# Heads between scores and probabilities, a section in two parts, scatters in parts, later small loads, output by halves

## The reference

```python
sh1, sc1, gt1, sh2, sc2, gt2 = split(silu(cond) @ w_mod[l] + b_mod[l], 6)
h = rmsnorm(x, g_mix[l]) * (1 + sc1) + sh1
aq, ak, av, mq, mk, mv, mo, mi, mf = split(h @ w_in[l])
att  = softmax(rope(norm(aq)) @ [cache_k, rope(norm(ak))].T / 8) @ [cache_v, av]   # 8 query, 2 key heads of 64
h_ml = mlstm_forward(mq, mk, mv, mi, mf) + mlstm_backward(...)                     # 4 heads of 128
x = x + gt1 * concat(att, sigmoid(mo) * rmsnorm(h_ml)) @ w_out[l]
h = rmsnorm(x, g_ffn[l]) * (1 + sc2) + sh2
gates = top-1 group of 4, then top-2 experts in it, of softmax(h @ w_router)
x = x + gt2 * sum_e gates_e * (silu(h @ w_gate[l,e]) * (h @ w_up[l,e])) @ w_down[l,e]   # 16 experts of 512
```

## Time and profile before

| | us |
|---|---|
| median of 3 runs | 891.59 (891.47 to 891.73) |
| the profiled execution | 891.36 |
| its span in the profile | 889.2 |
| PE busy | 837.6 (94% of the span) |
| DVE, ACT, POOL busy | 269.7, 179.6, 46.8 |
| chain that ended last: PE, DMA, DVE, ACT | 75%, 13%, 6%, 4% |

### The profile page before, as it was taken

How to read it: one execution, slowest core, us unless ns; L and a number is a source line. 1 busy time by engine, 2 the same in 40 slices (tenths; PEclk the granted TensorE clock), 3 DMA queues, 4 the chain that set the end, 5 groups by cost and what they waited for, 6 DMA issues and landing times.

```text
span 889.2 us, 10662 instructions
## 1 busy us (share of the span) xinstructions
PE 837.6 (94%) x4332; PEld 470.2 (53%) x4332; DVE 269.7 (30%) x503; ACT 179.6 (20%) x354; POOL 46.8 (5%) x51
## 2 busy tenths in 40 slices
PE   4899999998999999999989999989799999999996
PEld 3364647775444554355445555778553555345533
DVE  0211385425322122202230317652532022202222
ACT  3221224415101110011031212350510110011101
POOL 0400220101000000000000004000000000000000
PEclk9999999999999999999999999999699999999999
DMA  8995468859799999999999445705249999999981
GB/s 355 353 389 203 174 251 338 297 191 418 298 402 422 427 429 427 430 428 427 425 402 356 179 189 180 299 25 190 95 195 394 424 429 427 430 428 430 427 382 49
DMA packets 39763, 289.32 MB, mean 325 GB/s; under 512 B 3304, under 2 KB 5664, under 8 KB 21296
## 3 DMA queue, kind: packets, MB, share of 16 engines
q1 hardware_dynamic: 38000, 285.30, 78.9%
q0 software_dynamic: 1488, 3.44, 1.3%
q10 hardware_dynamic: 240, 0.08, 0.0%
HBM read 286.44 MB, written 2.37 MB: 325 GB/s over the span
## 4 chain that ended last, share of the span: by engine, by line
PE 75%; DMA 13%; DVE 6%; ACT 4%; issue 1%; SPq 1%; ACTq 0%; DVEq 0%
PE ps L965 22%; PE ps L639 13%; DMA ring<-in_w_e_up 10%; PE ps L993 9%; PE ps L885 6%; PE ps L953 6%; PE ps L1002 5%; DMA ring<-in_w_in 3%; PE ps L651 3%; PE ps L560 3%; PE ps L805 1%; PE ps L820 1%; ACT xe L1324 1%; DVE og L1543 1%; ACT hT L1150 1%
## 5 line engine op out<-in xcount | busy, mean ns | idle before, releaser
L965 PE MATMUL ps<-ring,xe 128*64 128x512 f32 x1024 | 223.5, 593 | 0.8 <-DMA ring<-in_w_e_up 0.6
L965 PEld LDWEIGHTS ps<-ring,xe 128*64 128x64 f32 x1024 | 75.2, 137 | 145.2 <-issue 145.0
L639 PE MATMUL ps<-ring,hT 128*128 128x512 f32 (+1 forms) x320 | 128.7, 563 | 4.1 <-DMA ring<-in_w_in 2.5
L993 PE MATMUL ps<-ring,hidT 128*64 128x512 f32 x512 | 113.4, 595 | 1.6 <-ACT hidT L1336 1.6
L639 PEld LDWEIGHTS ps<-ring,hT 128*128 128x128 f32 x320 | 62.1, 195 | 68.0 <-issue 59.1
L1754 DVE COPY ye<-ps 128x512 f32<-128x512 f32 x16 | 11.1, 692 | 215.0 <-PE ps L993 215.0
L953 PE MATMUL ps<-pick,htok 128*128 (+1 forms) x512 | 67.3, 288 | 7.4 <-ACT xe L1324 3.5
L993 PEld LDWEIGHTS ps<-ring,hidT 128*64 128x64 f32 x512 | 36.2, 137 | 67.4 <-issue 66.0
L953 PEld LDWEIGHTS ps<-pick,htok 128*128 128x128 f32 x512 | 64.1, 202 | 11.9 <-ACT xe L1324 6.8
L1002 PE MATMUL ps<-scat,ye 128*128 (+1 forms) x256 | 59.5, 385 | 1.8 <-DVE ye L1754 1.8
L1002 PEld LDWEIGHTS ps<-scat,ye 128*128 128x128 f32 x256 | 47.3, 190 | 20.6 <-issue 14.8
(11 more groups left out here) (258 smaller groups left out, 635.0 us busy)
## 6 DMA issues: line engine op xcount, KB each, us to landing
ring<-in_w_e_gate SPq DMA_DIRECT2D x32, 2048.0 KB, 13.9
ring<-in_w_e_up SPq DMA_DIRECT2D x32, 2048.0 KB, 17.0
ring<-in_w_e_down SPq DMA_DIRECT2D x32, 2048.0 KB, 12.1
ring<-in_w_mod SPq DMA_DIRECT2D x24, 2048.0 KB, 10.7
ring<-in_w_in SPq DMA_DIRECT2D x10, 2048.0 KB, 20.5
ring<-in_w_out SPq DMA_DIRECT2D x4, 2048.0 KB, 12.8
ring<-in_w_in SPq DMA_DIRECT2D x2, 1024.0 KB, 17.5
C<-in_state_C POOLq DMA_DIRECT2D x2, 512.0 KB, 7.6
```

Source lines behind the costliest of these rows:

```text
L639: mm = pe.matmul(bank[:, 0:width], hT[:, k, b * P:(b + 1) * P], w[:, k, :], start=(k == 0), stop=(k == KD - 1))
L965: mm = pe.matmul(ps[1 + u][64 * j:64 * j + 64, :], xe[:, k, j * SLOTS:(j + 1) * SLOTS], w[j][:, k, :], start=(k == 0), stop=(k == KD - 1))
L993: mm = pe.matmul(ps[3 - half][64 * j:64 * j + 64, :], hidT[:, k, j * SLOTS:(j + 1) * SLOTS], w[j][:, k, half * 512:(half + 1) * 512], star ...
```

## The change

1. The mLSTM heads move between the attention's scores and probabilities. On PE `own(0, 0..3)` comes ahead of the scores, `carried` and `own(1, .)` of heads 0 and 1 between s12 and s13, those of heads 2 and 3 behind the turned probabilities; `turn_heads(1)` and `turn_heads(0)` go behind the state, the second behind the fillers 6 and 7. DVE and ACT follow. The scaled `inter` values have three buffers in `hT` where they had two in `pT1`. The second reciprocal of DVE's gate goes behind `joined(3)`.
2. Layer 1's last section has two halves of 8 chunks: section 2 (scale 2) with two slots in the mixing stage (`filling` 0 and 4 only), and section 3 (gate 2) with two slots loaded behind `w_out` and used as filler in the router stage. An instruction is 256 wide instead of 512, and a slot has 16 instead of 8.
3. A scatter waits for the second half of ye only ahead of its fifth chunk; in the last pair its last two chunks go behind `turn_hidden`.
4. POOL's small loads wait for the first projection's weights instead of the fourth modulation slot. The first slot of section 0 is multiplied ahead of the norm sums.
5. The output is turned, copied and stored by halves of the features, four stores of 256 KB for two of 512 KB, the first halves as soon as two of the four residual parts are done.

The diff, cut to its core:

```diff
+SECTION_CHUNKS = {(l, s): (16 * s, 16) for l in range(DEPTH) for s in range(3)}
+SECTION_CHUNKS[1, 2], SECTION_CHUNKS[1, 3] = (32, 8), (40, 8)
+def section_slots(l, s):
+    return SECTION_CHUNKS[l, s][1] // 4
+def last_section(l):
+    return later_sections(l)[-1]
 def later_sections(l):
-    return ([(l, 1)] if l == 0 else []) + [(l, 2)] + ([(l + 1, 0)] if l + 1 < DEPTH else [])
+    return ([(l, 1)] if l == 0 else []) + [(l, 2), (l + 1, 0) if l + 1 < DEPTH else (l, 3)]
...
-        inter_s = pT1.ap().rearrange("p i j k t -> p (i j k t)")[:, 0:4 * (MD + 1)].rearrange("p (n d e) -> p n d e", n=2, d=2)
+        inter_s = hT.ap().rearrange("p k t -> p (k t)")[:, MH * TOK:MH * TOK + 6 * (MD + 1)].rearrange("p (n d e) -> p n d e", n=3, d=2)
...
@@ block.sync
-            for b, name in enumerate(("y_prompt", "y_sample")):
-                for half in range(2):
-                    taken(sp, ("out", 2 * b + half))
-                sp.dma_start(t[name][0], otok[:, b, :]).then_inc(y_out, 16)
+            for half in range(2):
+                for b, name in enumerate(("y_prompt", "y_sample")):
+                    taken(sp, ("out", 2 * half + b))
+                    c = slice(half * 512, half * 512 + 512)
+                    sp.dma_start(t[name][0][:, c], otok[:, b, c]).then_inc(y_out, 16)
@@ block.tensor
+                if l == 0:
+                    pe.wait_ge(cond_silu, 1)
+                    section_rows(0, 0, 0)
                 for i in range(4):
                     norm_sums(("ssq1", l), sq, 2 * l, (2 * i, 2 * i + 1), i == 0, i == 3)
...
-                        elif n % 2 == 0:
-                            section_rows(l, 2, n // 2)
+                        elif n in (0, 4):
+                            section_rows(l, 2, n // 4)
...
-                taken(pe, ("qT1", l), ("kT1", l))
-                for i in range(4):
+                for h in range(MH):
+                    own(0, h)
+                taken(pe, ("qT1", l), ("kT1", l))
+                for i in range(3):
+                    cross_scores(i)
+                if l == 0:
+                    section_columns(l, 1)
+                for h in range(2):
+                    carried(h)
+                    own(1, h)
+                cross_scores(3)
...
+                filling(5)
+                for h in range(2, MH):
+                    carried(h)
+                    own(1, h)
...
+                turn_heads(1)
                 filling(6, 7)
+                turn_heads(0)
...
-                if filler:
-                    section_rows(l + 1, 0, 0)
+                section_rows(*fill, 0)
                 pe.wait_ge(part_ready, l + 1)
...
-                        scatter(p - 1)
+                        scatter(p - 1, chunks=range(KD - 2 if last else KD))
                     turn_hidden(p)
-                    if not last:
+                    if last:
+                        scatter(p - 1, chunks=(KD - 2, KD - 1))
...
-            taken(pe, (("y", 3), DEPTH - 1))
             for r in range(4):
-                b, half = r // 2, r % 2
+                b, half = r % 2, r // 2
+                taken(pe, (("y", 2 * half + 1), DEPTH - 1))
@@ block.scalar
-                for i in range(6):
-                    exponent(i)
...
+                for i in range(3):
+                    exponent(i)
+                carry(0)
+                carry(1)
+                for i in range(3, 6):
+                    exponent(i)
...
+                for b in (1, 0):
+                    key = (f"oT{b}", l)
+                    bank = full(act, key)
+                    act.activation(cat[:, 0:4, b * P:(b + 1) * P], bank[:, :].rearrange("p (k t) -> p k t", k=4),
+                                   ACT.Copy).then_inc(free(key), 1)
                 act.activation(scrap[:, :], eps[:, :], ACT.Ln)
@@ block.vector
+                score_peaks(0, 1, 2)
+                if l == 0:
+                    modulation_columns(l, 1)
+                open_gate(1, 0, ML // 2)
+                score_peaks(3, 4, 5)
+                joined(0)
+                joined(1)
                 taken(dve, (("num", 0, MH - 1), l))
                 divisors(0)
-                joined(0)
-                joined(1)
+                 heads_out(0).then_inc(head_sum, 1)
                 joined(2)
                 joined(3)
+                open_gate(1, ML // 2, ML)
+                attended(1)
                 taken(dve, (("num", 1, MH - 1), l))
                 divisors(1)
...
                 dve.tensor_reduce(hr[:, 1, :], num[:, 1, :, 0, 0:MD], AX_X, ALU.add).then_inc(head_ssq, 1)
+                attended(0)
@@ block.gpsimd
-            pool.wait_ge(slot_landed[weights["mod", 0, 0, 3][0]], 16)
+            pool.wait_ge(slot_landed[weights["mk", 0][0]], 16)
```

More of the change, by code:

```diff
@@ L216, in put @@
         n += 1
-    for i in range(SEC_SLOTS):
+    for i in range(section_slots(0, 0)):
         put(("mod", 0, 0, i))
@@ L221, in weight_plan @@
         for sec in early_sections(l):
-            for i in range(SEC_SLOTS):
+            for i in range(section_slots(*sec)):
                 put(("mod", *sec, i))
@@ L467, in was_read, with load_section @@
                     full(sp, ((key[0], 1), key[1]))
-            def load_section(l, s, which=range(SEC_SLOTS)):
-                for i in which:
-                    load(("mod", l, s, i), w_mod[l, :, SEC_ROWS * i:SEC_ROWS * (i + 1), s * SEC:(s + 1) * SEC], k=SEC_ROWS)
+            def load_section(l, s, *which):
+                first, chunks = SECTION_CHUNKS[l, s]
+                n = section_slots(l, s)
+                k = KD // n
+                for i in which or range(n):
+                    load(("mod", l, s, i), w_mod[l, :, k * i:k * (i + 1), first * P:(first + chunks) * P], k=k)
             def load(key, src, width=WB, k=KD):
@@ L1352, in _ @@
                                        scale=-1.0).then_inc(spill_exp[l], 1)
-            for r in (0, 2):
+            for r in range(3):
+                b, half = r % 2, r // 2
                 bank = full(act, ("out", r))
-                act.activation(otok[:, r // 2, (r % 2) * 512:(r % 2 + 1) * 512], bank[:, :], ACT.Copy).then_inc(free(("out", r)), 1)
+                act.activation(otok[:, b, half * 512:(half + 1) * 512], bank[:, :], ACT.Copy).then_inc(free(("out", r)), 1)
         @block.vector
@@ L1603, in joined, with score_peaks @@
                     dve.tensor_tensor(num[:, 1, h, :, :].rearrange("p d e -> p (d e)"), bank[:, 0:2 * (MD + 1)],
-                                      inter_s[:, h % 2, :, :].rearrange("p d e -> p (d e)"), ALU.add).then_inc(free(key), 1)
+                                      inter_s[:, h % 3, :, :].rearrange("p d e -> p (d e)"), ALU.add).then_inc(free(key), 1)
+                def score_peaks(*which):
+                    for i in which:
+                        key = (f"s1{i}", l) if i < 4 else (f"s0{i - 4}", l)
+                        bank = full(dve, key)
+                        few = heads_of(i)
+                        dve.tensor_reduce(peaks[:, int(i < 4), few.start:few.stop:2],
+                                          bank[:, :].rearrange("p (h k) -> p h k", h=len(few)),
+                                          AX_X, ALU.max, negate=True).then_inc(score_max, 1)
@@ new lines, in spread, with attended @@
+                def spread(key, dst):
+                    bank = full(dve, key)
+                    dve.tensor_copy(dst, bank[:, 0:dst.shape[1]]).then_inc(free(key), 1)
+                def attended(b):
+                    for g in range(NKV):
+                        key = (f"o{b}{g}", l)
+                        o = full(dve, key)[:, 0:4 * (HD + 1)].rearrange("p (n d) -> p n d", n=4)
+                        share = shares[:, b, 4 * g:4 * g + 4]
+                        step(dve.reciprocal(share, o[:, :, HD]))
+                        dve.tensor_tensor(on[:, b, 4 * g * HD:4 * (g + 1) * HD].rearrange("p (n d) -> p n d", n=4), o[:, :, 0:HD],
+                                          per_col(share, HD), ALU.mult).then_inc(free(key), 1)
@@ L1798, in _ @@
                 residual(l, "y", 5)
-            for r in (1, 3):
-                bank = full(dve, ("out", r))
-                dve.tensor_copy(otok[:, r // 2, (r % 2) * 512:(r % 2 + 1) * 512], bank[:, :]).then_inc(free(("out", r)), 1)
+            bank = full(dve, ("out", 3))
+            dve.tensor_copy(otok[:, 1, 512:1024], bank[:, :]).then_inc(free(("out", 3)), 1)
         @block.gpsimd
```

211 lines of the change are left out of this document (87 added, 124 removed).

## The result

| | before | changed | ratio, 95% interval |
|---|---|---|---|
| first comparison, 4 runs each | 891.66 (891.47 to 892.43) | 881.44 (879.01 to 882.87) | 0.990 [0.9872, 0.9928] |
| second, beside the experiments, 35 and 12 runs | 889.71 (883.28 to 893.87) | 882.52 (880.41 to 891.56) | 0.9946 [0.9919, 0.9973] |

The kernel became faster: by 10 and 7 us between the medians, by 9 (6 to 11) and 5 (2 to 7) by the two ratios and their intervals. Its gain of 5.4 is too small by the first comparison and within the interval of the second. The second one, made for the experiments, shows that a run of this kernel is a draw: runs of the same kernel lie some 10 us apart, and the three runs behind "891.59" were no middle of them.

The account below looks back on a forecast made before the run. Expert weights were taken to pace the expert stages, and PE's work and few waits the rest. Terms -1.0 + 2.05 - 0.5 - 4.85 + 2.1 - 3.2 = -5.4 from 891.36 gave 886.0 profiled, median 886.2, range 883.6 to 889.8.

Parts of the forecast that it names:

- Nothing inside the expert stages pays: Expert stages: the weight stream sets the pace, so no gain there except behind the last landing.
- two added losses of 1.5 and 0.7 behind the new gaps: Slow clock after PE's idle time ahead of mlT: 1.5 us lost in layer 0, 0.7 more in layer 1.
- Start (-1.0): Up to the first projection: 1.0 us gained through item 4, ends 0 and 2.5.
- Layer 0's mixing stage (+2.05): Layer 0: mlT 0.55 us later behind ACT's table loads plus 1.5 of slow clock; ends gain 1.0, loss 3.5.
- Layer 1's mixing stage (-4.85): Layer 1: mlT 5.35 us sooner, 0.7 lost to slow clock, 0.2 gained on turns; ends 2.5 and 6.
- rival A: Layer 1's chain gains only its fillers' 2.5 us because ACT or DVE waits: 889.0; chance 0.16.
- Layer 1's router stage (+2.1): Layer 1's router stage: filler ahead of norm sums, row copy and turn lose 2.1 us; ends 0.7 and 2.9.
- Between the layers (-0.5): Layer 0's last pair to layer 1's projection: 0.5 us gained, limited by the weight stream; ends 0 and 1.6.
- End (-3.2): Kernel's end: sooner hidden turn, no ye wait, earlier and smaller last store gain 3.2 us; ends 2.3 and 3.8.
- B: Both mixing-stage gaps: the clock is not lost, or ACT gets the second turn sooner: 883.6; chance 0.11.
- C: Whole kernel: hardly any change, 890.5, or 889.0 with ACT's table-load drain; chance 0.13 including the drain.
- D: Layer 1's deferred expert loads make PE wait for two slots, 9.8 us: slower, 896.0; chance 0.05.

Follow-up runs that it names:

- before_again: The kernel before, unchanged, profiled a second time and timed again: 889.79 us, ratio 1.0006 to the kernel before.
- changed_again: The changed kernel, unchanged, profiled a second time with more timed rounds: 882.52 us, ratio 0.9946 to the kernel before.
- end_only: The kernel before with items 3 and 5 alone (scatters in parts, output by halves): 887.00 us, ratio 0.9974.
- router_slot: The changed kernel with layer 1's router-stage filler slots moved behind the norm sums and behind the router's logits: 880.02 us, ratio 0.9908 to the kernel before.
- power_early: The changed kernel with ACT's logarithm table loaded before its state copies and the second turned attention copied behind the power: 874.59 us, ratio 0.9837 to the kernel before.
- heads_and_split: The kernel before with items 1 and 2 together and nothing else: 886.56 us, ratio 0.9972.
- start_both: The kernel before with item 4 alone (POOL's small loads later, first slot ahead of the norm sums): 890.39 us, ratio 1.0017.
- start_pool: The kernel before with only POOL's small loads made to wait for the first projection's weights: 889.87 us, ratio 1.0009.

## Why the prediction was off

**What bounds the kernel.** Right in kind. PE is idle in the same few places, and no slot made it wait in layer 1's first pair. "Nothing inside the expert stages pays" held for what the edits do; the last stage's 1.15 is a draw.

**The base.** "The sum is made against its own time" (the profiled 891.36), and I took 0.2% for what a measurement can tell. In 88 later runs the kernel before has medians of 889.2 to 890.2 and, but for the one far off, goes from 883.1 to 894.2; twelve more reach 895.35. The three runs shown lay within 0.3 us of each other and 1.4 to 2.4 above these medians. A time worked out from them is too high by as much, and the range's low end of 883.6 with it. As a ratio the forecast (0.994) is within the second interval and outside the first.

**The step that failed: what half clock costs.** With two profiles of each kernel, the means can be set beside the sum (timeline):

| stretch | before | changed | difference | forecast |
|---|---|---|---|---|
| start to turn of mk, layer 0 | 117.37 | 114.82 | -2.55 | -1.0 |
| to gate products, layer 0 | 101.92 | 103.41 | +1.49 | +2.05 |
| to layer 1's first projection | 244.92 | 244.42 | -0.50 | -0.5 |
| to mlT, layer 1 | 126.52 | 121.21 | -5.31 | -5.35 |
| to gate products, layer 1 | 56.20 | 57.58 | +1.38 | +2.6 |
| to the end | 240.73 | 237.13 | -3.60 | -3.2 |

The sum priced the clock, apart from the start, at +0.5: two added losses of 1.5 and 0.7 behind the new gaps, and 1.7 saved in layer 1. PE's work at half clock in these profiles, added up over stretches of 1 us:

| | to turn of mk | to mlT | to gate products | layer 1 to mlT | to gate products |
|---|---|---|---|---|---|
| before | 6.8 | 0 | 3.4 | 3.4 | 16.3 |
| before_again | 3.4 | 0 | 6.0 | 3.4 | 16.1 |
| changed | 0 | 0 | 6.4 | 0 | 14.0 |
| changed_again | 3.4 | 0 | 6.5 | 1.6 | 14.3 |

Half of each figure is loss. Behind mk's turn it fell from 24.3 to 21.4 in the mean, a gain of 1.5 where the sum had a loss of 0.5. The largest part is layer 1's router stage: the sum added 0.7 for the clock behind mlT, and the stage has 1.0 less of loss than before. In layer 0 it is 0.9 more where the sum added 1.5. PE did run at half clock right behind both gaps; what failed is that this was added to the old profile's half clock as if all of that stayed. Ahead of mk's turn another 1.7 is a difference of draws, since kernels without item 4 show it as well. These are two profiles of each kernel: the sign is read from them, the size would need more.

**Start (-1.0).** Its sign is not borne out by the timed ratios, and its cause is not shown: the first projection starts 0.6 sooner on average with item 4, but at 32.6 in five of seven profiles without it.

**Layer 0's mixing stage (+2.05).** Its mechanism came out: ACT's copy, two table loads, mlT 0.74 later against mk's turn (46.35 for 45.61, forecast 0.55), the first mix part slow, +2.10 in all. From mk's turn to mlT every profile with the new order and the tables in their place takes 46.5 us; the old order takes 45.8 four times, and 47.4 to 47.5 three times, with a stretch at half clock. So in the mean mlT is no later. From mlT to the gate products it is 57.2 for 56.1, and PE's work right behind mlT is at half clock in all five of the new order and in one of seven of the old. The stage lost 1.1 in the mean over these profiles, not 2.05.

**Layer 1's mixing stage (-4.85).** By the chain -5.56. mlT came 5.3 to 5.5 sooner after its projections, forecast 5.35. The split of that was wrong: rival A priced the fillers alone at 2.5, and alone they gave nothing (126.44 for 126.52).

**Layer 1's router stage (+2.1).** Mis-sized: +1.07. The 1.36 of the norm sums measured 1.38; the row copy and the turn, priced at 0.6, cost 0.24 up to the gather and hid behind the ranks for the rest; and the gather took 0.55 less at a less low clock.

Together layer 1 takes 182.6 to 185.0 before (six profiles with the old order and section) and 178.5 to 179.1 after: -5.4 in the mean, -3.9 by the two kernels' own profiles, where the sum has -2.75. Timed, items 1 and 2 in both layers gave 2.5 us (0.2 to 4.8), and the sum had 0.7 for them. So the sign of this miss is shown by the profiles, its size is open.

**Between the layers (-0.5)** measured -0.1 and -0.7 in the changed kernel's two profiles, but `end_only` and `router_slot`, which have item 3 too, took longer than either profile of the kernel before (245.10 and 245.38 for 244.81 and 245.03): not told from nothing. **End (-3.2)** measured -3.63: 0.79 for hidden, 0.08 in the products, 0.90 for ye, 0.87 for the output, and 0.99 behind the last copy, where I had 0.6.

**Rivals.** B's number (883.6) came nearest, by luck: it rests on the clock not being lost behind the gaps, and it was lost there (0.62 and 0.50). A, C and D fell. The Trainium skill (ScalarE: Activation LUTs, "What ACT_TABLE_LOAD costs") counts a drain of about 1.38 us with every switch; in `power_early` the exponential follows its load after 0.02 us (154.26 and 1.28, then 155.56), so here too no drain shows.

**Open.** The profiles' spans give the change 9 us in the mean, the timed medians 7 to 10, the ratios 5 to 9. Where a stretch at half clock falls in an execution I can read, not foretell, and no experiment here moved one at will. The ratios of `heads_and_split`, `end_only` and `start_both` multiply to 0.996, each with an interval of some 0.002 on either side; the whole has 0.9946 and 0.990.

## What to carry to other kernels

Ask first how far single executions lie apart, and with what they go: here a thousandth of mean granted clock was worth about 1.1 us, and three equal runs hid a spread of ten. Keep PE's idle time, which repeats, apart from a stage's length, which doesn't. A low clock is a cost only where PE has work, so do not add a slow stretch behind a new gap without asking which old one goes. And look at what an engine's row puts ahead of its table loads: moving one load ahead and one copy behind was worth about as much as the whole change.

## What the runs showed of the hardware

- Stretches at half clock stand in all 14 profiles, also where PE was at work throughout (4.00 us busy of 4.00 at 0.57), and some at other places from one execution to the next (layer 0's mixing stage in `start_pool`, its gather in `before_again`). From the first projection to mk's turn in layer 0 each cost 1.7 us (81.4, 83.1 and 84.8 us with none, one and two).
- The first projection's weights held PE until 34.2 and 35.4 us in two of the seven profiles with early small loads on POOL's queue, and until 32.6 in five (released by the weights or by ACT's result); until 32.5 to 32.8 in all seven without them. The cause of the two is open.
- PE stood idle 1.11 us with its data ready at the end of one program, and not in another with the same instructions there.
